# Two-block transformer on one core: a Silu, two PSUM copies and a transpose change their places

## The reference

```python
zxbcdt = x @ w_in                       # gate z (4096), xbc (6144), dt (64)
xbc = silu(causal_conv4(xbc) + conv_b)  # xs (4096), B (1024), C (1024)
dt = softplus(dt_raw + dt_bias); a = -exp(a_log)
# per head, in chunks of 128 tokens, da_cum = cumsum(dt * a):
cb       = C @ B.T                               # per group of 8 heads
decay_in = exp(da_cum[q] - da_cum[s]) for s <= q
y        = (cb * decay_in) @ (xs * dt) + terms across chunks + xs * d_skip
y = y * silu(z); y = rms_norm per group * norm_w; out = y @ w_out
```

## Time and profile before

| | |
|---|---|
| runs, us | 2203.01, 2201.77, 2200.43; median 2201.77 |
| the profiled execution | 2200.1 us, span of its records 2198.0 us |
| mean granted PE clock | 0.994 of full speed |
| PE busy | 2147.5 us, 98% of the span, 12110 matmuls |
| DVE busy | 1359.1 us, 62% |
| ACT busy | 1084.5 us, 49% |
| DMA | 403.08 MB, mean 183 GB/s |
| the chain that ended last | PE 90%, DVE 4%, ACT 3%, issue 2% |

### The profile page before, as it was taken

How to read it: one execution, slowest core, us unless ns; L and a number is a source line. 1 busy time by engine, 2 the same in 40 slices (tenths; PEclk the granted TensorE clock), 3 DMA queues, 4 the chain that set the end, 5 groups by cost and what they waited for, 6 DMA issues and landing times.

```text
span 2198.0 us, 32627 instructions
## 1 busy us (share of the span) xinstructions
PE 2147.5 (98%) x12110; PEld 1852.5 (84%) x12110; DVE 1359.1 (62%) x1660; ACT 1084.5 (49%) x1420; POOL 133.8 (6%) x142
## 2 busy tenths in 40 slices
PE   8999999999999999999899999999999999999999
PEld 8988889998887778998788878778888888888887
DVE  5677776776545667765676665655555655554554
ACT  4444457776343455763454465544434434443442
POOL 2000001111000100000014300000000000000000
PEclk9999999999999999999999999999999999999999
DMA  7577766565655554457476544455656656656654
GB/s 234 183 191 205 217 192 178 169 182 159 225 193 191 191 178 142 140 180 215 151 212 207 172 144 138 148 180 165 190 194 188 187 196 187 189 192 188 190 191 161
DMA packets 207162, 403.08 MB, mean 183 GB/s; under 512 B 16228, under 2 KB 18404, under 8 KB 206772
## 3 DMA queue, kind: packets, MB, share of 16 engines
q1 hardware_dynamic: 199168, 385.92, 56.2%
q0 software_dynamic: 4192, 14.50, 3.0%
q10 hardware_dynamic: 3668, 0.73, 0.2%
HBM read 395.27 MB, written 5.83 MB: 182 GB/s over the span
## 4 chain that ended last, share of the span: by engine, by line
PE 90%; DVE 4%; ACT 3%; issue 2%; POOL 1%; DMA 0%; DVEq 0%; SPq 0%; ACTq 0%
PE ps L401 16%; PE ps L402 16%; PE ps L403 15%; PE ps L385 15%; PE ps L387 8%; PE ps L372 5%; PE ps L373 5%; PE ps L374 5%; ACT whi L354 1%; PE ps L1157 1%; DVE wlo L359 1%; PE ps L1250 1%; PE ps L1327 1%; PE ps L1431 1%; PE ps L1350 1%
## 5 line engine op out<-in xcount | busy, mean ns | idle before, releaser
L359 DVE TENSOR_TENSOR wlo<-raw,whi 128x1024 fp32r<-128x1024 f32 x712 | 875.4, 1234 | 743.4 <-ACT whi L354 739.3
L354 ACT ACTIVATE whi<-raw 128x1024 fp32r<-128x1024 f32 x712 | 753.7, 1060 | 1033.2 <-PE ps L403 583.4
L385 PE MATMUL ps<-xhl,whi 128*128 128x512 f32 x1472 | 519.2, 398 | 6.2 <-DVE cumc L1583 2.8
L387 PE MATMUL ps<-xhl,wlo 128*128 128x256 f32 x1472 | 413.6, 281 | 0.0
L385 PEld LDWEIGHTS ps<-xhl,whi 128*128 128x128 f32 x1472 | 276.8, 188 | 74.8 <-DVE wlo L359 4.4
L372 PE MATMUL ps<-xhl,whi 128*128 128x256 f32 x1088 | 316.7, 291 | 10.7 <-DVE wlo L359 10.7
L401 PE MATMUL ps<-whi,xhl 128*128 128x512 f32 x792 | 319.7, 404 | 2.4 <-ACT nkT L963 1.7
L402 PE MATMUL ps<-wlo,xhl 128*128 128x512 f32 x792 | 310.1, 392 | 0.0
L403 PE MATMUL ps<-whi,xhl 128*128 128x512 f32 x792 | 310.0, 391 | 0.0
L373 PE MATMUL ps<-xhl,whi 128*128 128x256 f32 x1088 | 308.8, 284 | 0.0
L374 PE MATMUL ps<-xhl,wlo 128*128 128x256 f32 x1088 | 308.6, 284 | 0.0
(11 more groups left out here) (242 smaller groups left out, 1997.2 us busy)
## 6 DMA issues: line engine op xcount, KB each, us to landing
raw<-w SPq DMA_DIRECT2D x256, 512.0 KB, 4.3
raw<-w_in SPq DMA_DIRECT2D x160, 512.0 KB, 4.4
raw<-w_qkv SPq DMA_DIRECT2D x96, 512.0 KB, 4.3
raw<-w_out SPq DMA_DIRECT2D x64, 512.0 KB, 4.3
raw<-b_in SPq DMA_DIRECT2D x64, 512.0 KB, 3.7
raw<-b_out SPq DMA_DIRECT2D x32, 512.0 KB, 4.2
raw<-w_o SPq DMA_DIRECT2D x32, 512.0 KB, 3.7
cumb<-cum_scratch SPq DMA_DIRECT2D x16, 512.0 KB, 4.2
```

The costliest lines, as they stand in the source:

```text
L354: act.activation(whi[:, u % RING], raw[:, u % RING], ACT.Copy).then_inc(S("hi_ready"), 1)
L359: dve.tensor_tensor(wlo[:, u % RING], raw[:, u % RING], whi[:, u % RING].bitcast(F32), ALU.subtract).then_inc(S("lo_ready"), 1)
L385: pe.matmul(ps[:, bank + n, :], whi[:, u % RING, t, n * P:(n + 1) * P], both, start=(k == 0), stop=False, skip_group_check=True)
L387: last = pe.matmul(ps[:, bank + n, 0:T], wlo[:, u % RING, t, n * P:(n + 1) * P], xh[:, k, :], start=False, stop=(k == KT - 1), skip_group_ ...
```

## The change

Three edits. ACT: the Silu of panel 11 moves from ahead of the first decays to the end of gate group 0, ahead of that group's gate rows. DVE: the copies of `dtt` and `cumc` move from behind the splits of units 28 to 35 to ahead of them. PE and DVE: the second turn of group 0 comes after unit 99 instead of unit 98, and DVE takes up its scaling after splitting unit 101 instead of unit 102.

```diff
@@ ACT, before the gate stage
             for i in range(BC_PANELS + 1, n):
                 low_half(i - 1)
                 silu_panel(i, (i - (BC_PANELS + 1)) * NB)
-            silu(n - 1, XS_TILES - NB)
@@ ACT, gate stage
                     if j % 2 == 0 and PAIRS * g + j // 2 + 1 < PAIRS * GROUPS:
                         decays(PAIRS * g + j // 2 + 1)
+                if g == 0:
+                    silu(CONV_PANELS - 1, XS_TILES - NB)
                 gate_rows(g)
@@ PE, group(g)
                     feature_unit(pe, Z + g * UPP + j, 0, j, Z_BANKS[g % 2], xh, xl)
-                    if g == 0 and j == 2:
+                    if g == 0 and j == 3:
                         acc_free(1, CONV_DIM // PANEL // 2)
                         inputs_turned(0, 1)
@@ DVE, xbc stage
-            conv_panel(2, 0, 0, B_TILE0 + 2 * NB, True)
+            conv_panel(2, 0, 0, B_TILE0 + 2 * NB, False)
             dve.wait_ge(S("dtt_mm"), 1)
             dve.tensor_copy(dtt[:].rearrange("p a b -> p (a b)"), ps[:, 5, 0:2 * SSM_HEADS])
             dve.tensor_copy(cumc[:].rearrange("p a b -> p (a b)"), ps[:, 5, 2 * SSM_HEADS:4 * SSM_HEADS])\
                .then_inc(S("cumc_ready"), 1)
+            for c in range(UPP):
+                split_lo(dve, RING + UPP * 3 + c, 0)
             dve.wait_ge(S("cumc_ready"), 1)
@@ DVE, gate stage
                     split_lo(dve, Z + g * UPP + RING + j, 0)
-                    if g == 0 and j == 2:
+                    if g == 0 and j == 1:
                         inputs_scaled(0, 1)
```

## The result

In the first comparison the changed kernel took 2188.61 us (median of six runs, 2187.28 to 2192.28) against 2200.79 for the kernel before: ratio 0.9946, 95% interval 0.9936 to 0.9956. The forecast was 2195.5 in a range of 2192.8 to 2199.3, so the direction was right and the gain, 12.2 us, nearly twice the 6.3 forecast. Over all series, this first one included, the means are 2201.04 us (106 runs of the kernel before, standard error 0.21) and 2190.47 (22 runs of the changed kernel, 0.47): 10.6 us, of which the forecast holds 6.3. The first six runs of the changed kernel were a little fast (mean 2188.99, against 2191.03 for the 16 later ones).

What follows compares the result with a forecast made beforehand. PE, busy 98% of the span, was taken as the bound, so only its waits could be won. Gains of 2.9 and 4.0 less 0.6 give 6.3 us, from median 2201.77 to 2195.5 us; range 2192.8 to 2199.3.

Steps and rivals of the forecast that it cites:

- Edit 1: DVE copies of dtt and cumc ahead of eight splits: PE's wait before wide unit 32 goes, gaining 2.9 us.
- thin cover at unit 36: Slack of unit 36's split on DVE ahead of PE's need: falls from 3.4 to 0.9 us, thin but enough.
- Edits 2 and 3: Group 0, Silu moved to its end and second turn a unit later: three PE waits go, gaining 4.0 us.
- new wait at `states(1)`: In group 0, PE would wait 0.1 to 0.26 us for DVE's masked product before states(1).
- the chain of ACT and DVE: Group 0: ACT does decays and unit 100's high half during DVE's convolution; DVE splits unit 100 from 304.8 to 306.0.
- The Silu's price: At the Silu's new place, unit 108's high half and group 1's first y pair start later, costing 0.6 us.
- No table load was added: After unit 103 ACT loads the Silu table in either version, so moving the Silu adds no load.
- the sum, 2.9 + 4.0 - 0.6: Gain from the copies, plus gain in group 0, less the moved Silu's cost: 6.3 us in all.
- only time in which PE stands still can be won: PE is busy 98% of the span, so a change moving no matmul work is worth its effect on PE's waits.

Runs made afterwards that it cites:

- silu_earlier: Changed kernel with the Silu one split earlier and states(1) of group 0 behind unit 99 and the turn; ratios 0.9944 and 0.9946, mean 2190.3 us.
- before_again: The kernel before, unchanged, profiled a second time; 2200.07 us.
- before_timed: The kernel before, unchanged, timed like a changed kernel against its own runs; ratio 0.9992, mean 2199.87 us.
- neutral_memset: The kernel before with one more memset on DVE early in the first panel, which PE does not wait for; ratio 0.9998.
- waits_filled: The kernel before with its PE waits kept but filled with matmuls whose results nothing reads; ratio 0.9980, mean 2197.35 us.
- turn_only: The kernel before with only group 0's second turn and its scaling moved, Silu and copies left in place; ratio 0.9986, median 2198.17 us.

## Why the prediction was right in its mechanism and wrong in its size

- *Edit 1, forecast 2.9.* Right: 2.96 at unit 32. The thin cover at unit 36 held: its low half started at 118.10, PE had no wait.
- *Edits 2 and 3, forecast 4.0.* Right: C shows 3.73 net; with the 0.50 of the next point 4.2. The new wait at `states(1)` was 0.26, the upper of its two ends, the chain of ACT and DVE as worked out to 0.3 us.
- *The Silu's price, forecast 0.6.* Right: 0.50 by its row, and silu_earlier gets it back. No table load was added, and the load took 1.28 us. The Trainium skill's 2.66 us for a switch (ScalarE: Activation LUTs, What ACT_TABLE_LOAD costs) does not fit here: the Silu starts 1.30 us after the load starts.
- *The failed step is the sum, 2.9 + 4.0 - 0.6.* I set the gain of a wait equal to its length: "only time in which PE stands still can be won". What the clock does after PE has stood still I put at nothing without giving a reason: behind the waits it fell to 1.2 GHz in a part of the executions. By the profiles this took 0.9 to 1.5 us each time at unit 32 (B against 159.03, the mean of the ten profiles without it), in five of seven, and 1.4 in group 0, in three of six: 1.5 us in the mean. With the 6.7 of the waits that makes 8.2, and the four profiles of before, before_again, before_timed and neutral_memset against the four of the changed kernel show 8.5 up to the end of the gate stage, the first units included.
- *How far that goes.* Measured are 10.6 (error 0.5), so some 2 us are not explained. waits_filled, at 3.7 (error 0.8) with every wait in place, would close the gap (6.7 + 3.7 = 10.4), but for the reason given there the agreement may be luck.
- *What I could have seen.* The profile that I had read shows a grant of 1.00 in both places, and I took one execution's clock for the kernel's. The Trainium skill has the rule (TensorE: Matmul & The Clock Gate, What's actually happening): an idle TensorE falls back to half its clock. The traces agree for the 2.80 us wait in five of seven profiles, and in two the clock stayed up. I should have carried it as a rival with its own price.
- *The rest of the first result, 12.2 against 10.6,* is the draw of six runs (and the medians: by their means they are 11.8 apart). The 4.2 us in the MLP quarters belong to the two profiled executions alone.

Open: where the remaining 2 us are. Behind the gate stage, where no edit is, the four profiles against four differ by a further 3.9 us, but the two profiles of `silu_earlier` are the longest of all sixteen there, so that can be chance. One count is worth knowing: the first quarter was slow in six of the eight profiles with the Silu at its old place and in one of the eight with it moved. At 1.7 us each that would be 1.1 us (an estimate); whether it is more than chance no run here shows. Whether the clock falls more often where no profile is taken I can't tell either, nor why turn_only is timed 3.5 us faster (error 0.9) at a C of 40.43; an offset of about 1 us between a series and its comparison would cover a part of it.

## What to carry to other kernels

Price a wait of the matmul engine as its length plus a chance of a lowered clock behind it, and look at more than one profile before you take that chance for zero. To separate the two, fill the wait with matmuls into an unused bank, and time the unchanged kernel beside it as if it were a changed one: here it came out 1.6 us (error 0.8) from its own comparison. When two edits serve one chain, only the one that frees its slowest engine counts alone: the Silu moved was worth 3.17 us, the turn moved 0.

## What the runs showed of the hardware

In the first half of an MLP quarter the wide pair (512 columns, then 256) runs at one of two paces at a granted clock of 1.00, and keeps it to the half's end: 88.73 or 90.43 us for 512 matmuls. Forty microseconds of the third quarter, before and then after:

```profile
1850.00:1890.00 40.00, 40.00 (x228) 34.65 (x227) 22.59 (x19) 17.71 (x18) 0.00 (x0) 1.00 0.61 186
```

```profile
1841.00:1881.00 40.00, 40.00 (x233) 34.93 (x232) 23.20 (x20) 18.79 (x19) 0.00 (x0) 1.00 0.61 184
```

In 16 profiles the slow pace came in 11 of 48 quarters (the second to fourth of each), with and without the edits. What chooses it is open. At 1.7 us for each slow quarter it may be a good part of why single runs of the kernel before lie between 2194.6 and 2206.2 us; no run here separates it.
